# First norm's modulation in four quarters, each fetched with a quarter of the first projection's weights, and nine filler matmuls ahead of that projection

## What is computed

```
sh1, sc1, g1, sh2, sc2, g2 = split(silu(c) @ w_ada + b_ada)     # and the same for c_ctx
hc = rms_norm(ctx, norm_mix) * (1 + csc1) + csh1                # 256 context tokens
s_f, s_b = states of the context from hc @ w_in[:, 512:2048]
hx = rms_norm(x, norm_mix) * (1 + sc1) + sh1                    # 512 tokens
q, zf_f, zf_b, i, g, gate_b, gate_c, v = split(hx @ w_in)
```

## Time and profile before

| | before |
|---|---|
| median of 3 runs | 2088.63 us (2087.45 to 2089.3) |
| the profiled execution | 2088.94 us, of which its span 2087.2 us |
| mean granted clock of TensorE | 0.992 |
| TensorE busy | 2003.7 us, 96% |
| VectorE, ScalarE busy | 901.1 us, 576.9 us |
| transfers | 529.58 MB, mean 254 GB/s |

### The profile page before, as it was taken

One profiled execution on the slowest core, in us unless ns is written; L12 is line 12 of the kernel. 1 busy time (PEld: TensorE's weight loads), 2 busy tenths in 40 slices (PEclk: granted clock), 3 DMA queues, 4 the chain that ended last, 5 costly groups with the idle time before them and its releaser, 6 DMA issues.

```text
span 2087.2 us, 23788 instructions
## 1 busy us (share of the span) xinstructions
PE 2003.7 (96%) x9892; PEld 1249.9 (60%) x9892; DVE 901.1 (43%) x1479; ACT 576.9 (28%) x901; POOL 58.2 (3%) x107
## 2 busy tenths in 40 slices
PE   7999999999999899999999998999999999999998
PEld 5888777543533334242433333776688888888886
DVE  4666683320111111111101101877897656767555
ACT  5434322100100000000000001537725343334445
POOL 1000010000000000000000000005300000000000
PEclk9999999999999999999999999999999999999999
DMA  9462126899999999999999999142132232232322
GB/s 352 161 230 93 41 74 290 355 409 400 430 429 430 430 431 414 429 430 430 430 431 430 430 430 420 52 140 41 41 112 90 81 121 81 88 115 81 111 79 83
DMA packets 111100, 529.58 MB, mean 254 GB/s; under 512 B 15398, under 2 KB 44178, under 8 KB 83346
## 3 DMA queue, kind: packets, MB, share of 16 engines
q1 hardware_dynamic: 110993, 528.07, 62.8%
HBM read 525.95 MB, written 2.10 MB: 253 GB/s over the span
## 4 chain that ended last, share of the span: by engine, by line
PE 90%; DMA 5%; DVE 3%; issue 2%; ACT 0%; SPq 0%; POOL 0%; ACTq 0%; DVEq 0%
PE bank L1090 22%; PE bank L645 12%; PE bank L646 12%; PE bank L647 12%; PE bank L1174 8%; DMA f<-in_w_gate_dram 3%; PE bank L1047 3%; PE bank L1064 3%; PE bank L652 3%; PE bank L654 3%; PE bank L656 3%; PE bank L666 2%; PE bank L1279 1%; PE bank L1388 1%; DMA f<-in_w_in_dram 1%
## 5 line engine op out<-in xcount | busy, mean ns | idle before, releaser
L1090 PE MATMUL bank<-f,high 128*64 128x512 f32 x2048 | 465.3, 602 | 28.7 <-issue 13.2
L645 PE MATMUL bank<-r 128*128 128x512 f32 x920 | 363.5, 395 | 3.4 <-DVE r L2105 2.7
L646 PE MATMUL bank<-r 128*128 128x512 f32 x920 | 359.1, 390 | 0.0
L647 PE MATMUL bank<-r 128*128 128x512 f32 x920 | 359.1, 390 | 0.0
L1090 PEld LDWEIGHTS bank<-f,high 128*64 128x64 f32 x2048 | 148.7, 138 | 315.6 <-issue 298.3
L1174 PE MATMUL bank<-f,high 128*64 128x512 f32 x1024 | 228.0, 601 | 7.8 <-issue 7.8
L2442 DVE SCALAR_TENSOR_TENSOR f<-bank,low,f 128x512 f32<-128x512 f32 x64 | 48.0, 750 | 400.6 <-PE bank L1064 400.2
L1520 ACT ACTIVATE high<-bank 128x512 f32<-128x512 f32 (+3 forms) x95 | 52.0, 579 | 565.5 <-PE bank L666 271.2
L407 DVE TENSOR_TENSOR r<-f,r 128x1024 fp32r<-128x1024 f32 (+2 forms) x167 | 190.8, 1195 | 32.2 <-ACT r L401 32.1
L645 PEld LDWEIGHTS bank<-r 128*128 128x128 f32 x920 | 172.4, 187 | 46.0 <-issue 5.5
L647 PEld LDWEIGHTS bank<-r 128*128 128x128 f32 x920 | 172.3, 187 | 37.6
(11 more groups left out here) (390 smaller groups left out, 2062.1 us busy)
## 6 DMA issues: line engine op xcount, KB each, us to landing
f<-in_w_up_dram SPq DMA_DIRECT2D x58, 2048.0 KB, 20.4
f<-in_w_down_dram SPq DMA_DIRECT2D x56, 2048.0 KB, 20.3
f<-in_w_gate_dram SPq DMA_DIRECT2D x55, 2048.0 KB, 18.9
f<-in_w_up_dram SPq DMA_DIRECT2D x34, 1024.0 KB, 7.3
f<-in_w_in_dram SPq DMA_DIRECT2D x13, 2048.0 KB, 7.7
f<-in_w_down_dram SPq DMA_DIRECT2D x22, 1024.0 KB, 12.1
high<-in_w_ada_dram SPq DMA_DIRECT2D x32, 512.0 KB, 5.5
f<-in_w_gate_dram SPq DMA_DIRECT2D x16, 1024.0 KB, 10.7
```

What stands on the lines that cost most here:

```text
L645: pe.matmul(o, wh, xh, start=first, stop=False)
L646: pe.matmul(o, wl, xh, start=False, stop=False)
L647: return pe.matmul(o, wh, xl, start=False, stop=last)
L1090: ins = pe.matmul(o[64 * e:64 * e + 64, :], xsT[p % 2][:, 2 * k + r, 64 * e:64 * e + 64], ws[e](2048 * r + 512 * fc), start=k == 0 and r = ...
```

## The change

- w_ada's shift and scale columns are fetched in eight transfers of 256 columns (1 MB, rows of 1 KB) in place of four of 512. The order is zf0, scale0, shift0, zf1, scale1, shift1 and so on; quarter q serves the channels of tiles d = 2q and 2q + 1.
- TensorE does all token transposes first, then quarter 0's columns and turn, then nine f32 matmuls of 256 columns into bank 3 whose result nobody reads, then the projection. The columns of quarters 1, 2 and 3 stand in the middle of k = 0, 2 and 4, their turns ahead of k = 1, 3 and 5.
- ScalarE splits zf0 ahead of the token copies, and goes quarter by quarter (copy, rounding of two tiles). The squares and the root of the context and `a_divide(VI)` come behind the rounding of all eight tiles.
- VectorE splits zf0 ahead of its token copies and goes quarter by quarter too.
- SP waits for the columns of quarter 2 ahead of chunk 1; the third and fourth buffer of the later w_ada rows wait for quarter 1's columns.

```diff
@@ sync (SP)
-        ada_at = [M + 18432, slot_at[3], M + 14336, slot_at[2]]
-        ada_order = (2, 0, 3, 1)
-        early = [own(4096, a_) for a_ in ada_at]
+        early = [own(4096, a_).rearrange("p (a k n) -> p a k n", a=2, k=8)
+                 for a_ in (M + 14336, M + 18432, slot_at[2], slot_at[3])]
+        SHIFT, SCALE = range(2)
...
-            load_ada(2)
-            load_ada(0)
-            load_chunk(0)
-            load_ada(3)
-            load_ada(1)
+            def ada_part(a, q):
+                return I["w_ada"][0][:, D * a + 256 * q:D * a + 256 * q + 256].rearrange("(k p) n -> p k n", p=P)
+
+            for q in range(4):
+                load_chunk(ZF, [q])
+                sp.dma_start(early[q][:, SCALE], ada_part(SCALE, q)).then_inc(s[f"scale{q}"], 16)
+                sp.dma_start(early[q][:, SHIFT], ada_part(SHIFT, q)).then_inc(s[f"shift{q}"], 16)
...
-            sp.wait_ge(s["pe_ada"], val("pe_ada", 3))
-            sp.wait_ge(s["pe_ada"], val("pe_ada", 1))
+            sp.wait_ge(s["pe_ada"], val("pe_ada", 2))
             load_chunk(1)
...
-                        sp.wait_ge(s["pe_ada"], val("pe_ada", 0))
+                        sp.wait_ge(s["pe_ada"], val("pe_ada", 1))
@@ tensor (TensorE)
+            def ada_columns(q, *bs):
+
+                key = ("ada", q)
+                o = claim(bs[0], key, "adatmp", q) if bs else take(key, "adatmp", q)
                 pe.wait_ge(s["a_pre"], val("a_pre", "cp"))
-                for k in range(8):
-                    ins = pe.matmul(o[32 * (k % 4):32 * (k % 4) + 32, :], CP[:, k, :], w[:, k, :], start=k < 4, stop=k >= 4)
-                up(ins, "pe_ada", c)
+                for a, landed_ in ((SCALE, f"scale{q}"), (SHIFT, f"shift{q}")):
+                    pe.wait_ge(s[landed_], 16)
+                    z = slice(256 * a, 256 * a + 256)
+                    for k in range(8):
+                        ins = pe.matmul(o[32 * (k % 4):32 * (k % 4) + 32, z], CP[:, k, :], early[q][:, a, k, :],
+                                        start=k < 4, stop=k >= 4)
+                up(ins, "pe_ada", q)
...
-            tokens_turned(0)
-            tokens_turned(1)
-            ada_columns(ada_order[0])
-            tokens_turned(2)
-            ada_turned(ada_order[0])
-            ada_columns(ada_order[1])
-            tokens_turned(3)
-            ada_turned(ada_order[1])
+            for t in range(4):
+                tokens_turned(t)
+            ada_columns(0)
+            ada_turned(0)
+            pe.wait_ge(s["consts"], val("consts", "ones256"))
+            after(3)
+            for _ in range(9):
+                pe.matmul(banks[3][:, 0:256], ident, ones256, start=True, stop=True)
...
             for k in range(8):
-                if k == 2:
-                    ada_columns(3, 0)
-                    ada_columns(1, 1)
-                if k == 3:
-                    ada_turned(3, 2)
-                    ada_turned(1, 3)
+                q, odd = k // 2 + 1, k % 2
+                if odd and q < 4:
+                    ada_turned(q, 2)
                 weights(ZF, k, 8)
                 pe.wait_ge(s["uh"], val("uh", k))
                 pe.wait_ge(s["ul_v"], val("ul_v", k))
                 for j in range(4):
+                    if j == 2 and not odd and q < 4:
+                        ada_columns(q, q % 2)
@@ scalar (ScalarE)
+            a_divide(a, ZF, [0])
             for t in range(4):
-                if t == 3:
-                    a_divide(a, ZF, [0])
-                if t > 1:
-                    ada_tmp(ada_order[t - 2])
...
-            a_divide(a, ZF, [1])
-            rounded_tokens((0, 1, 2, 3))
-            a_divide(a, ZF, [2])
-            ada_tmp(3)
-            ada_tmp(1)
-            a_divide(a, ZF, [3])
+            for q in range(4):
+                ada_tmp(q)
+                if q == 0:
+                    a_divide(a, ZF, [1])
+                rounded_tokens((2 * q, 2 * q + 1))
+                if q < 2:
+                    a_divide(a, ZF, [q + 2])
             a.wait_ge(s["ctx"], 16)
...
             up(a.activation(ss[:, 4:6], ss[:, 4:6], ACT.Sqrt, bias=epst, scale=1.0 / D), "a_pre", "rc")
-            rounded_tokens((4, 5, 6, 7))
             a_divide(a, VI)
@@ vector (VectorE)
+            v_divide(v, ZF, [0])
             for t in range(4):
-                if t == 3:
-                    ada_bias(ada_order[0])
-                    v_divide(v, ZF, [0])
...
-            modulation(0)
-            v.wait_ge(s["a_pre"], val("a_pre", "xt", 3, 0))
-            modulated(0)
...
-            token_rest(6)
-            token_rest(7)
+            for q in range(4):
+                ada_bias(q)
+                modulation(q)
+                if q == 0:
+                    v.wait_ge(s["a_pre"], val("a_pre", "xt", 3, 0))
+                modulated(2 * q)
+                modulated(2 * q + 1)
+                token_rest(2 * q)
+                token_rest(2 * q + 1)
+                if q == 0:
+                    v_divide(v, ZF, [1])
+                if q < 2:
+                    v_divide(v, ZF, [q + 2])
```

More of the change, by code:

```diff
@@ L18 @@
 NEG = -1e30
-DMA_SEMS = (*(f"g{i}" for i in range(6)), *(f"cg{i}" for i in range(4)), *(f"zf{i}" for i in range(4)), "x0", "x1", "rows0", "rows", "small", "ctx", "wple", "ada0", "ada1", "ada2", "ada3", "w0", "w1", "ptok", "gf", "out",
+DMA_SEMS = (*(f"g{i}" for i in range(6)), *(f"cg{i}" for i in range(4)), *(f"zf{i}" for i in range(4)), "x0", "x1", "rows0", "rows", "small", "ctx", "wple", *(f"scale{i}" for i in range(4)), *(f"shift{i}" for i in range(4)), "w0", "w1", "ptok", "gf", "out",
             *(f"m{i}" for i in range(9)), "mx", "my", "mg0", "mg1", "mh0", "mh1", "mq0", "mq1")
@@ L435, in sync, with load_chunk @@
         def sync(sp):
-            def load_chunk(c):
+            def load_chunk(c, pieces=None):
                 for i, (dst, src) in enumerate(chunks[c][0](whole(c))):
+                    if pieces and i not in pieces:
+                        continue
                     sp.dma_start(dst, src).then_inc(s[{ZF: f"zf{i}", CG: f"cg{i}"}.get(c, f"w{pair[c]}")], 16)
@@ L691, in tensor, with ada_turned @@
             up(pe.transpose(o[:, 0:128], stage[:, 0, :], ident), "pe_pre", "pt")
[L693 to L698, removed]
-                pe.wait_ge(s["a_pre"], val("a_pre", "cp"))
-                for k in range(8):
-                    ins = pe.matmul(o[32 * (k % 4):32 * (k % 4) + 32, :], CP[:, k, :], w[:, k, :], start=k < 4, stop=k >= 4)
-                up(ins, "pe_ada", c)
-            def ada_turned(c, *bs):
-                o = claim(bs[0], ("adaT", c), "adaT", c) if bs else take(("adaT", c), "adaT", c)
-                pe.wait_ge(s["adatmp"], val("adatmp", c))
+            def ada_columns(q, *bs):
+                key = ("ada", q)
+                o = claim(bs[0], key, "adatmp", q) if bs else take(key, "adatmp", q)
+                pe.wait_ge(s["a_pre"], val("a_pre", "cp"))
+                for a, landed_ in ((SCALE, f"scale{q}"), (SHIFT, f"shift{q}")):
[5 more added lines that the diff above has]
+                up(ins, "pe_ada", q)
+            def ada_turned(q, *bs):
+                o = claim(bs[0], ("adaT", q), "adaT", q) if bs else take(("adaT", q), "adaT", q)
+                pe.wait_ge(s["adatmp"], val("adatmp", q))
                 pe.wait_ge(s["consts"], val("consts", "sel"))
-                t = adatmp[ada_order.index(c) % 2]
+                t = adatmp[q % 2]
                 for j in range(4):
                     ins = pe.matmul(o[:, 2 * j:2 * j + 2], t[:, 128 * j:128 * j + 128], sel, start=True, stop=True)
-                up(ins, "pe_ada", "T", c)
+                up(ins, "pe_ada", "T", q)
             def tokens_turned(t):
@@ L1520, in copy, with ada_tmp @@
                 return a.activation(o, i, ACT.Copy)
[L1522 to L1527, removed]
+            def ada_tmp(q):
+                a.wait_ge(s["pe_ada"], val("pe_ada", q))
+                if q > 1:
+                    a.wait_ge(s["pe_ada"], val("pe_ada", "T", q - 2))
+                up(copy(adatmp[q % 2], bank("ada", q)[:, :]), "adatmp", q)
             done = {g: [] for g in range(1, 6)}
@@ L2073, in add_squares, with ada_bias, modulation @@
                 up(ins, "sqs", g, d)
-            def ada_bias(c):
-                v.wait_ge(s["pe_ada"], val("pe_ada", "T", c))
+            def ada_bias(q):
+                v.wait_ge(s["pe_ada"], val("pe_ada", "T", q))
                 v.wait_ge(s["v_pre"], val("v_pre", "pt"))
-                bb = col["b_ada"][:, 4 * c:4 * c + 4].unsqueeze(2).to_broadcast([P, 4, 2])
-                up(v.tensor_tensor(adaT[:, 4 * c:4 * c + 4, :], bank("adaT", c)[:, 0:8].rearrange("p (t r) -> p t r", r=2),
-                                   bb, ALU.add), "adaT", c)
+                z = slice(2 * q, 2 * q + 2)
+                bb = v3(col["b_ada"][:, 0:16], 2)[:, :, z].unsqueeze(3).to_broadcast([P, 2, 2, 2])
```

(13 more changed lines are left out.)

22 lines of the change are left out of this document (removed).

## The result

| | before | changed |
|---|---|---|
| median | 2088.7 us (6 runs, 2087.45 to 2090.23) | 2097.06 us (6 runs, 2096.26 to 2098.39) |
| the profiled execution | 2088.94 us, span 2087.2 | 2096.65 us, span 2094.9 |
| ratio | | 1.0039, 95% interval 1.0029 to 1.0049 |

The change makes the kernel 8.4 us slower (the interval of the ratio is 6.1 to 10.2 us). The forecast was 2095.6.

A forecast was written before the change was run, and what follows sets the result against it. TensorE, busy 96% of the span, was taken as the bound. ScalarE's wait 5.3 + clock 1.7 = +7.0 us on span 2087.2, plus 1.7 outside it, less 0.3 to the median: 2095.6; range 2090.5 to 2100.5.

The forecast's parts named there:

- the deciding term: ScalarE's late squares, chunk 1 and context copy hold TensorE's small-row transposes until 64.7 us, 5.3 us later than 59.45.
- the inside of the projection: First projection: 22.0 us of matmuls, 8.7 of column groups and turns, 0.2 of switching; no wait for transfers.
- the clock behind the wait: After TensorE's 5.6 us idle ahead of the small rows, a lowered clock costs 1.7 us, bounds 0 and 3.4.
- the start: Transposes end at 18.6 us and the first projection starts at 26.3, 0.7 us earlier than before.
- rival 2: In the opening, transposes keep TensorE at 1.2 GHz, so all behind moves by 1.5 us: 2097.1, up to 2099.9; chance 0.28.
- the clock saved at the start: Fillers leave no idle ahead of the first projection, so its first 24 matmuls run at full pace, saving 1.7 us.
- the 4.1 us: Three table loads on ScalarE's new path, each with a 1.38 us drain by the skill's rule, would give 2099.7.
- what happens behind the opening: After 60 us, a delay of TensorE reaches the end in full, with no slack to swallow it.

The follow-up runs named there:

- the short delay: Kernel before plus twelve f32 filler matmuls (5.2 us) on TensorE ahead of VI's first token tile, at 60 us; 2095.03 us against 2089.5.
- the fillers alone: Kernel before plus six filler matmuls (2.6 us) between the second turn and the first projection; 2088.62 us against 2089.02.
- two pure delays: Kernel before plus twelve or 24 f32 filler matmuls on TensorE at 60 us; 2095.03 us against 2089.5, and 2100.4 against 2088.86.
- the early squares: Changed kernel with the context's squares and root behind the rounding of tiles 4 and 5, ahead of the fourth quarter's copy; 2090.31 us against 2089.5.
- the small rows later: Changed kernel, squares early, five fillers, small rows' transposes behind VI's second token tile, VectorE reordered to match; 2086.86 us against 2089.02, again 2087.76 against 2088.86.
- the long delay: Kernel before plus 24 f32 filler matmuls (10.4 us) on TensorE ahead of VI's first token tile, at 60 us; 2100.4 us against 2088.86.
- both repairs: Changed kernel with the context's squares and root early and five fillers instead of nine; 2089.1 us against 2089.02.

## Why the prediction was right, step by step

**Right: the deciding term.** The forecast worked ScalarE's chain from the end of the last turn to the small rows as 2.25 + 3.92 + 6.80 + 2.69 = 15.7 us. Measured: 47.52 to 63.01, 15.5 us, piece by piece nearly the same (squares to root 3.92, chunk 1 to the sigmoids' load 6.81). TensorE's idle was forecast as 5.6 us and is 5.39. Taking the cause away and setting it alone into the kernel before showed it twice. ScalarE's order was the bound though it is busy 28% of the span: the share says nothing of the 15 us in which TensorE's next work hangs on it.

**Right: the inside of the projection**, 30.9 us forecast, 30.8 measured (24.94 to 55.71). No quarter waits for a transfer: shift0 landed at 16.1 (16.8 forecast), chunk 1 at 48.2 and was wanted at 53.5. The transfers, 1 KB rows with the 2 KB rows of ZF among them, ran at 384 to 402 GB/s from 12 to 24 us, as the w_up row said.

**Right, partly by luck: the clock behind the wait**, 1.7 forecast, 1.6 measured in the first execution and 2.1 in the second (6.6 at the modulation rows less 4.5 at the small rows). The 1.7 was borrowed from another gap, of half the length. Behind waits of 5.39 and 5.42 us the kernels without fillers and with five took 132.18 and 132.00 us to the modulation rows instead of 129.42, so the cost was 1.6 to 2.8 us in four executions.

**Mis-sized: the start.** I took the transposes to end at 18.6 and the projection to start at 26.3. They ended at 17.3, the columns began at once, and the start was 24.94. The term is the 6.7 us for 32 transposes, which took 5.02 to 6.21 us in the eight executions with this order. The pace rises in their midst. Hence for the most part the shift of the small rows was 3.6 us and not 5.3 (4.5 in the second execution).

**Wrong rival: the late full pace.** By rival 2 transposes keep TensorE at 1.2 GHz. The stretches of the changed kernel show it false: in 12 to 14 us TensorE did ten transposes, in 14 to 16 us fourteen, before it had done anything but transposes. The counts tell it here: the granted clock reads 1.00 in 12 to 16 us, and it did so before too, where 16 transposes took 3.67 us.

```profile
12.00:14.00 2.00, 2.00 (x10) 2.00 (x11) 2.00 (x4) 1.99 (x5) 0.00 (x0) 1.00 1.09 386
14.00:16.00 2.00, 2.00 (x14) 2.00 (x13) 2.00 (x3) 0.67 (x2) 0.00 (x0) 1.00 1.09 402
16.00:18.00 2.00, 2.00 (x28) 1.57 (x30) 1.64 (x3) 1.20 (x2) 0.00 (x0) 1.00 1.06 384
```

The kernel with the short delay shows it in the order of before. Its first 16 transposes took 3.27 us, and the column group behind them was at full pace from its first matmul:

```profile
11.88 3.27 PE L666 MATMUL bank<-low,high 128*128 128x128 f32 x16 [1.57 <-DVE high L2066]
15.08 1.92 PE L701 MATMUL bank<-f,low 128*32 128x512 f32 x16
```

The granted clock itself shows it in the changed kernel at the reload of x. From 328.50 us, behind 2.25 us of idle, TensorE does 32 transposes and nothing else for 5.38 us. The clock is 0.50 in 330 to 332 us, 0.63 in 332 to 333 and 1.00 in 333 to 334.

The Trainium skill ("TensorE: Matmul & The Clock Gate", "Part 4: PE-mode transpose") says that transposes do not bring the engine to its full rate. For these f32 transposes the measurement decides against it, and with it rival 2's 2097.1, which happens to lie on the measured time for another reason. The Trainium skill ("ScalarE: Activation LUTs", "What ACT_TABLE_LOAD costs") gives 2.66 us for a switch. Here the activation stands 1.29 us behind the start of the load each time (52.00 to 53.29, 57.40 to 58.69, 59.02 to 60.31), and the 4.1 us that the prediction estimated from that rule are not there.

**Wrong in its reason: the clock saved at the start, "so 1.7 us are saved".** It was credited against a projection end of before that the last modulation piece held, as the fillers alone showed. In the sum it did no harm: the end of before was taken from the trace (56.55) and the new one built up anew, so the credit was never added twice.

**Not in the sum: what happens behind the opening.** I carried the delay through unchanged. The two pure delays confirm that within 0.3 us of 5.2 and 1.1 of 10.4. Yet the two profiled executions of the changed kernel end 7.7 and 9.6 us later than that of before, against 5.2 and 6.6 at the modulation rows. That the forecast for the first came so near (+7.0 for +7.7) is luck in part: the opening was put 1.8 us too high, and 2.5 us behind it were put at nothing. In the first execution 1.3 of them arise at the reload of x. The stretch of the changed kernel, then that of the kernel with five fillers:

```profile
319.00:334.00 15.00, 12.75 (x75) 11.49 (x74) 7.44 (x12) 5.98 (x11) 0.00 (x0) 0.89 1.02 430
```

```profile
319.00:334.00 15.00, 12.34 (x79) 10.68 (x78) 8.00 (x13) 5.92 (x13) 0.00 (x0) 1.00 1.03 430
```

In both TensorE has a gap of two us there (2.25 and 2.20), as before had (1.91); in the first a stretch at the 1.2 GHz level follows, in the second none, and in before none. Five of the thirteen profiled executions have such a stretch (0.89 to 0.91 over these 15 us): both of the changed kernel, the short delay, the early squares, and the first of the small rows later. The other eight had none, and among them is the second execution of the small rows later, the same program (1.00), so it comes and goes with the execution. (In the long delay the gap falls later, at 332 to 334 us; the clock is 1.00 from 334 to 346.)

From the modulation rows to the end the kernel before took 1898.3 us. The five executions with the stretch took 0.9 to 3.0 us more, the seven others from 0.9 less to 1.2 more. The kernels without fillers and with five have all the transfers and the late squares of the changed kernel, and took 0.2 and 0.4 us less than before. So I count the rest as chance of the execution and not as a price of the change. That both executions of the changed kernel had the stretch leaves this argued and not proven, and the interval of the 8.4 us (6.1 to 10.2) holds the opening's cost of the second execution with nothing added.

## What to carry to other kernels

Work that is moved to a later place in an engine's queue has to be priced by what stands behind it until the bound engine's next wait, not by its length or by that engine's share of busy time. Splitting a step in more parts puts the last part later, and all that the same engine does behind the last part with it; look for the idle time between the parts and fill it with that work. Size fillers by the gap: five covered it, nine outlasted it by 1.4 us, and without any the clock was lost. Where a wait of TensorE stays behind work that now ends earlier, look at the clock behind it. With both repairs the wait was 2.04 us instead of 1.57, the clock fell, and the 1.6 us gained ahead of it were lost.

## What the runs showed of the hardware that I had not expected

TensorE came to its full pace while it did nothing but f32 transposes: 32 of them took 5.31 us at the start, where all at half pace would have been 7.3, and at the reload of x the granted clock went from 0.50 to 1.00 in the midst of 32 transposes. And the same 2 us gap at the reload of x was followed by a half-pace stretch in some executions and in others not, worth 1.3 us of a 2090 us kernel in the one compared with before. The executions of one kernel lie up to 5 us apart (the kernel before 2087.16 to 2091.53 in 32 runs, the early squares 2088.30 to 2093.26 in 11); one such stretch is a part of that.
